# A two-block transformer kernel on one core: both halves of X in one product for the feature-major chunks, with a two-engine evacuation

## The chip, the cores and the metric

The kernel runs on one core of one Trainium2 chip. The core has TensorE (PE in the profile, with its weight loads as PEld), VectorE (DVE), ScalarE (ACT), GpSimd (POOL) and SyncE (SP, which here only issues DMAs). The metric is the device time of one execution in microseconds (us); lower is better. All names L823 and the like are line numbers of the kernel before.

## The reference

One sequence of 256 tokens, width 1024, goes through three layers, all in fp32. The parts that matter here:

```
mix = token_mixer(x)            # q,k,v of 8 forgetting heads (FoX) and 8 banded heads; w_out
  FoX: logit[t,s] = q_t.k_s/8 + cum[t] - cum[s], s <= t,  cum = cumsum(log_sigmoid(f + b_forget))
x   = layer_norm(a1*x + mix)
u   = x @ w_up ; u = conv over 3 tokens ; x = layer_norm(a1*x + (value*gelu(gate)) @ w_down)
h   = x @ w_in_even             # retention q,k,v,gate (4 heads) and MLA q,kv,gate (8 heads)
x   = layer_norm(a2*x + concat(ret_out, mla_out) @ w_out_even)
h   = x @ w_in_odd              # q,k,v,gate of 16 heads, rotary, causal within 256 tokens
x   = layer_norm(a2*x + (attention * silu(gate)) @ w_out_odd)
```

A softmax over s does not change when a term that depends on t alone is added to its logits, so `cum[t]` may be left out.

## The kernel before, in words

**Products in three parts.** An fp32 matrix product is made of three fp32r products: each operand is split into `hi` (its value rounded to fp32r by a ScalarE copy) and `lo` (value minus `hi`, a VectorE subtraction), and hi·hi, hi·lo and lo·hi are added up in PSUM (`three`, L823 to L825). The activations stand feature-major in `X_hi`, `X_lo` (8 tiles of 128 features by 256 tokens) and, for the input of an output projection, in `S_hi`, `S_lo`.

**Weights as a stream of pieces.** All weights are cut into 236 pieces, most of them 128x1024. SP loads a piece into one of 5 `raw` slots, ScalarE makes `w_hi` of it (L1117), VectorE `w_lo` (L1283), in a ring of 6, and TensorE uses it and frees it. A piece is split four pieces ahead of its use.

**Chunks.** Pieces form chunks (`chunks()`). A chunk of kind F makes 128 output features per piece with all 256 tokens as moving columns: 8 tiles times three matmuls of 256 columns, weights stationary. Up to two pieces share one PSUM bank. Kinds A and B have tokens as the stationary side and weights as 512 moving columns. `acc` has four banks for chunks, which rotate, and four more (`job`) for attention, transposes and retention. Before its first matmul a chunk waits until what its banks held has been evacuated (`chunk_waits`).

**Evacuation of an F chunk** is one step (`evac`): q and k of the first layer are copied by ScalarE (L1156); the convolution of a `w_up` chunk is two scaled ScalarE reads of PSUM (`taps`, L1125) and four VectorE multiply-adds that read PSUM (L1326); a rotary chunk is rotated by VectorE straight from PSUM (L1307 to L1318); a gate is a ScalarE tanh (L1171) and a VectorE multiply-add (L1346), both from PSUM.

**Attention** goes in pairs of heads through four steps each (`scores`, `soft`, `exp`, `norm`, then `pt`, `pv`, `yout`, `ylo`). For the FoX heads the term `cum[t] - cum[s]` enters as a second small product of 4 rows (L949) on top of q·k (L940). `cum` is computed in the `forget` evacuation: VectorE adds the bias (L1372), ScalarE does Abs, Exp and Ln (L1189), VectorE a minimum, a scan and four scalings (L1375 to L1383).

**The order** is one list (`plan`): half a piece of matmuls, the splits that belong to it, then at most one or two background steps. Each engine works through its own part of this list in order and waits on semaphores. A rotated chunk counts as ready four half pieces after its evacuation (`TURN_WAIT`).

Of the kernel before, what the change touches and what calls it, by code (L numbers as in the profile page):

```python
# [25 lines left out]
P = 128  # L26
# [40 lines left out]
def chunks():  # L67
# [29 lines left out]
    add("out1", "B", 8, "S", k8, "dve", ("norm", 0), ("w_out", k8, None))  # L97
# [11 lines left out]
    def mla(half):  # L109
        for a in (0, 1):  # L110
            add(f"mg{half}{a}", "F", 2, "X", k8, "dve", ("gate", 0, a),
                ("w_in_even", None, cols(MG + 512 * half + 256 * a, 256)), after_job=16 + 4 * half, at=2 + a)
# [45 lines left out]
    def moba_qk(half, a):  # L158
        for name, c0 in (("k", 1024), ("q", 0)):
            add(f"m{name}{half}{a}", "F", 2, "X", k8, "dve", ("rope", name, 1 - half, 2 * a, 64),  # L160
                ("w_in_odd", None, [c0 + 512 * half + 256 * a + 64 * h + i for h in range(4) for i in turn_perm]), after_ret=4)

    def moba_gate(half, a):
        add(f"mgt{half}{a}", "F", 2, "X", k8, "dve", ("gate", 1 - half, a),
            ("w_in_odd", None, cols(3072 + 512 * half + 256 * a, 256)), after_ret=4)
# [11 lines left out]
    add("out3", "B", 8, "S", k8, "dve", ("norm", 3), ("w_out_odd", k8, None))  # L177


    width = dict(F=1, A=2, B=4, C=4, Q1=4, Q2=4)  # L180
# [65 lines left out]
def cum_row(h):  # L246
    return 64 * (h % 2) + 32 * (h // 2 % 2)


# [8 lines left out]
def plan():  # L258

    order, given, pending, turning = [], set(), [], []  # L260
# [13 lines left out]

    def require(names):
        while not names <= given:
# [17 lines left out]
    def evacuate(c):  # L294
        emit(("evac", c))
        if CH[c]["evac"][0] in ("rope", "mla_q"):
            turning.append([CH[c]["name"], TURN_WAIT])
        else:
            given.add(CH[c]["name"])

    def run(name, rate, needs=lambda i: set(), early=0, between=(), tail=(), inside={}):
# [13 lines left out]
        for x, half in enumerate(halves):  # L315
# [25 lines left out]
            else:  # L341
                split_to(u + AHEAD + 1)
            for t in turning:
# [69 lines left out]
    split_to(1)  # L413

    for name in ("f", "kA0", "qA0", "vA", "kA1", "kB0"):
        run(name, 0)
# [10 lines left out]
    for j in range(2, FT + 2):  # L427
        if j < FT:
            run(f"up{j}", 0, tail=first if j == 2 else ())
# [53 lines left out]
    run("out3", 1, lambda i: {f"L3y{i}"})  # L483
# [59 lines left out]
for _name, _n in (("ident", P), ("causal", 3 * P), ("band", P), ("cumA", 4), ("cumB", 4),  # L543
# [6 lines left out]
def constants():  # L550
# [34 lines left out]
def build(nc, t):  # L585
    with ExitStack() as ctx:
# [9 lines left out]
        X_hi = sb("X_hi", [P, KT, S], F32R)  # L596
        X_lo = sb("X_lo", [P, KT, S], F32R)
# [77 lines left out]
        x_in = [sem(f"x_in{i}") for i in range(2 * NT)]  # L675
        pos_in, bf_in, conv_in = sem("pos_in"), sem("bf_in"), sem("conv_in")
# [23 lines left out]
        ROPES = [c for c, ch in enumerate(CH) if ch["evac"][0] in ("rope", "mla_q")]  # L700
# [1002 lines left out]
```

## Time and profile before

| | us |
|---|---|
| runs before (3): median, lowest, highest | 767.89, 767.82, 768.12 |
| the profiled execution's own time | 768.47 |
| its span | 766.7 |
| TensorE busy | 752.5 (98%) |
| VectorE busy | 528.8 (69%) |
| ScalarE busy | 382.5 (50%) |

The profiled execution is 0.58 us above the median of the runs. Its granted TensorE clock was 1.00 in nearly every stretch. Durations of matmuls overlap (each ends later than the next one starts), so the time that one matmul takes from TensorE is read as the distance between starts. Stages by time: first layer's q, k, v to 48 us, its attention and output projection to 150, `w_up` to 260, `w_down` to 330, the retention and MLA layer to 620, the last layer from there.

### The profile page before, as it was taken

To read this page: it belongs to the slowest core of one execution; us is meant where nothing else is said; L and a number is where in the kernel's file an instruction comes from. 1 tells how busy PE (TensorE), PEld (TensorE's weight loads), DVE (VectorE), ACT (ScalarE), POOL (GpSimd) and SP (SyncE) were. 2 spreads that over 40 slices of the span, in tenths; PEclk is the share of its full clock that TensorE was granted. 3 is DMA by queue.
4 is the path that set the end of the run, shared out by engine and by line. 5 is a ranking of instruction groups with operands and counts; after the bars stand their busy time and mean duration, and the time that the engine had idled before them with its cause. 6 is when DMAs were issued, how large, how long until landed. Compare 5 with 4: busy or idle time off the path is not lost.

```text
span 766.7 us, 12680 instructions
## 1 busy us (share of the span) xinstructions
PE 752.5 (98%) x4838; PEld 659.6 (86%) x4838; DVE 528.8 (69%) x940; ACT 382.5 (50%) x629; POOL 36.8 (5%) x50
## 2 busy tenths in 40 slices
PE   8999999999999999999999999999999999999995
PEld 8897777899999988799899777987788879988964
DVE  4654758697788854857686566965574587977766
ACT  5655763575655654156554444433443434565450
POOL 0000000021111200100000000000000010000001
PEclk9999999999999999999999999999999999999998
DMA  8852345456655685265536334553576617446402
GB/s 304 316 192 89 114 155 199 165 162 190 188 183 165 212 295 194 69 221 192 165 109 196 126 133 138 161 185 129 185 264 200 221 52 233 136 133 196 162 2 82
DMA packets 37580, 130.62 MB, mean 170 GB/s; under 512 B 4304, under 2 KB 4688, under 8 KB 37392
## 3 DMA queue, kind: packets, MB, share of 16 engines
q1 hardware_dynamic: 36144, 125.09, 49.2%
q0 software_dynamic: 1232, 4.46, 1.9%
q8 instruction: 39, 0.64, 0.3%
q10 hardware_dynamic: 144, 0.26, 0.1%
q14 instruction: 21, 0.17, 0.1%
HBM read 128.74 MB, written 1.05 MB: 169 GB/s over the span
## 4 chain that ended last, share of the span: by engine, by line
PE 95%; DVE 3%; issue 1%; DMA 1%; ACT 0%; DVEq 0%; SPq 0%
PE acc L823 28%; PE acc L825 27%; PE acc L824 27%; PE acc L940 2%; PE acc L959 2%; PE acc L979 2%; PE acc L998 1%; PE acc L938 1%; PE acc L1011 1%; PE acc L946 1%; DMA res<-in_x 1%; PE acc L972 0%; PE acc L1022 0%; PE acc L1037 0%; PE acc L1035 0%
## 5 line engine op out<-in xcount | busy, mean ns | idle before, releaser
L1283 DVE TENSOR_TENSOR w_lo<-raw,w_hi 128x1024 fp32r<-128x1024 f32 (+1 forms) x223 | 260.8, 1197 | 70.1 <-ACT w_hi L1117 69.3
L1117 ACT ACTIVATE w_hi<-raw 128x1024 fp32r<-128x1024 f32 (+1 forms) x223 | 224.4, 1034 | 88.8 <-PE acc L825 77.6
L823 PE MATMUL acc<-X_hi,w_hi 128*128 128x256 f32 x848 | 243.0, 287 | 0.6 <-DVE w_lo L1558 0.6
L824 PE MATMUL acc<-X_lo,w_hi 128*128 128x256 f32 x848 | 239.8, 283 | 0.0
L825 PE MATMUL acc<-X_hi,w_lo 128*128 128x256 f32 x848 | 239.8, 283 | 0.0
L823 PEld LDWEIGHTS acc<-X_hi,w_hi 128*128 128x128 f32 x848 | 162.5, 192 | 6.3 <-issue 5.1
L824 PEld LDWEIGHTS acc<-X_lo,w_hi 128*128 128x128 f32 x848 | 162.6, 192 | 0.5 <-issue 0.2
L825 PEld LDWEIGHTS acc<-X_hi,w_lo 128*128 128x128 f32 x848 | 162.5, 192 | 0.0
L823 PE MATMUL acc<-w_hi,S_hi 128*128 128x512 f32 x256 | 101.7, 397 | 1.3 <-DVE gate L1346 1.3
L824 PE MATMUL acc<-w_lo,S_hi 128*128 128x512 f32 x256 | 99.8, 390 | 0.0
L825 PE MATMUL acc<-w_hi,S_lo 128*128 128x512 f32 x256 | 99.7, 390 | 0.0
L823 PE MATMUL acc<-w_hi,X_hi 128*128 128x512 f32 (+1 forms) x192 | 74.4, 388 | 0.9 <-DVE w_lo L1283 0.9
L825 PE MATMUL acc<-w_hi,X_lo 128*128 128x512 f32 (+1 forms) x192 | 71.6, 373 | 0.0
L824 PE MATMUL acc<-w_lo,X_hi 128*128 128x512 f32 (+1 forms) x192 | 71.4, 372 | 0.0
L823 PEld LDWEIGHTS acc<-w_hi,S_hi 128*128 128x128 f32 x256 | 48.1, 188 | 13.0 <-issue 1.8
L825 PEld LDWEIGHTS acc<-w_hi,S_lo 128*128 128x128 f32 x256 | 48.1, 188 | 10.1
L824 PEld LDWEIGHTS acc<-w_lo,S_hi 128*128 128x128 f32 x256 | 48.1, 188 | 9.6 <-issue 0.2
L1326 DVE SCALAR_TENSOR_TENSOR v<-acc,cvp,v 128x255 f32<-128x255 f32 (+1 forms) x88 | 38.3, 477 | 20.9 <-ACT v L1125 20.1
L823 PEld LDWEIGHTS acc<-w_hi,X_hi 128*128 128x128 f32 x192 | 36.2, 189 | 9.4 <-issue 3.9
L1125 ACT ACTIVATE v<-acc,cvp 128x256 f32<-128x256 f32 x44 | 22.3, 561 | 42.6 <-PE acc L825 38.4
L825 PEld LDWEIGHTS acc<-w_hi,X_lo 128*128 128x128 f32 x192 | 36.2, 188 | 6.6
L824 PEld LDWEIGHTS acc<-w_lo,X_hi 128*128 128x128 f32 x192 | 36.3, 189 | 6.0 <-issue 0.5
(165 smaller groups left out, 795.7 us busy)
## 6 DMA issues: line engine op xcount, KB each, us to landing
raw<-in_w SPq DMA_DIRECT2D x225, 512.0 KB, 4.3
raw<-in_w SPq DMA_DIRECT2D x11, 256.0 KB, 3.1
gate<-in_ln_gain POOLq DMA_DIRECT2D x4, 512.0 KB, 5.2
gate<-in_ln_bias POOLq DMA_DIRECT2D x4, 512.0 KB, 5.7
res<-in_x SPq DMA_DIRECT2D x4, 256.0 KB, 4.2
gate<-in_bias SPq DMA_DIRECT2D x1, 1024.0 KB, 10.3
out<-res SPq DMA_DIRECT2D x4, 256.0 KB, 2.0
decay<-in_decay SPq DMA_DIRECT2D x1, 512.0 KB, 6.1
```

The lines of the kernel that those rows point to most:

```text
L823: nc.tensor.matmul(out, a_hi, b_hi, start=start, stop=False)
L824: nc.tensor.matmul(out, a_hi, b_lo, start=False, stop=False)
L825: return nc.tensor.matmul(out, a_lo, b_hi, start=False, stop=stop)
L938: nc.tensor.matmul(dst, qT[s][:, h, q], kT[s][:, h, 0:nk], start=True, stop=False)
L940: last[i] = nc.tensor.matmul(dst, qT[s][rows, h // 2, q], kT[s][rows, h // 2, 0:nk], start=True, stop=kind != "fox")
L946: last[i] = nc.tensor.matmul(dst, qpeT[rows, h // 2, q], kpeT[rows, 0, 0:nk], start=False, stop=True)
L959: last = nc.tensor.transpose(job[:, 2 + j % 2, b * P:(b + 1) * P], pr[:, j % 2, b * P:(b + 1) * P], ident)
L979: last = nc.tensor.matmul(job[i * HD:(i + 1) * HD, 3, q0:q0 + n], vv[s][:, tt, v], ptb[:, (j + i) % 2, b0:b0 + n], start=tt == 0, stop=tt ...
L1117: nc.scalar.activation(home(u, "hi")[:, 0:n], raw[:, u % RAW, 0:n], ACT.Copy).then_inc(hi_done, 1)
L1125: return [nc.scalar.activation(conv[j % 2][:, i, :], up[:, i * S:(i + 1) * S], ACT.Identity, scale=cvp[:, 2, i, j:j + 1], bias=cvp[:, 3, i ...
L1283: nc.vector.tensor_tensor(home(u, "lo")[:, 0:n], raw[:, u % RAW, 0:n], home(u, "hi")[:, 0:n].bitcast(F32), ALU.subtract).then_inc(lo_done, 1)
L1326: last = nc.vector.scalar_tensor_tensor(o, up[:, i * S:i * S + S - lag], cvp[:, 2 - lag, i, j:j + 1], o, ALU.mult, ALU.add)
```

## The change

- **Kind W.** `X_hi` and `X_lo` become the two halves of one tensor `X` (tile, half, token). For 48 chunks of two pieces (96 pieces) the kind F is replaced by W: per tile one matmul of 512 columns (`w_hi` on both halves) and one of 256 (`w_lo` on the hi half) instead of three of 256. A piece now has a bank of its own: columns 0 to 255 hold hi·hi and lo·hi, columns 256 to 511 hold hi·lo. A W chunk takes two of the four banks. The 48 chunks (in the code the same replacement stands in `ret_qk`, `moba_qk`, `moba_gate` and the second half of `mla`) are 6 of q and k of the first layer, 20 of `w_up`, 2 MLA gates, 8 of retention's q and k, 8 rotary and 4 gate chunks of the last layer. The single-piece chunks and the first two MLA gates stay F.
- **Evacuation of a W chunk.** At its end ScalarE copies the second halves of both banks to SBUF (`half`); half a piece later VectorE adds the first halves (`add_half`), which frees the banks. The convolution's taps and multiply-adds, the rotation and the tanh then read SBUF; a gate's tanh goes to another buffer and a further step (`gated`) multiplies.
- **FoX.** The product of 4 rows goes. The negated, scaled `cum` of the eight heads is written to DRAM and read back to all partitions by GpSimd's DMA queue (twice 512 KB), the causal mask is added by VectorE (`fox_mask`, four operations), and `soft` takes this as its bias. The scan moves behind the next chunk's third half piece (`forgotten`).
- **Order.** `rv0`, `out1`, `out3` start at bank 2 (`at=2`); `out3` takes its first two pieces token half by token half (`early=2`). At the start the second half of piece 0 is loaded and split before the last two parts of x. A ready rotary chunk counts five half pieces, not four.

```diff
-        add(f"{name}{half}", "F", 2, "X", k8, "act", ("copy_feat", name[0], s, 2 * half, 2),
+        add(f"{name}{half}", "W", 2, "X", k8, "dve", ("copy_feat", name[0], s, 2 * half, 2),
...
-        add(f"up{j}", "F", 2, "X", k8, "dve", ("conv", j),
+        add(f"up{j}", "W", 2, "X", k8, "dve", ("conv", j),
...
+    add("out3", "B", 8, "S", k8, "dve", ("norm", 3), ("w_out_odd", k8, None), at=2)
...
+        if CH[c]["kind"] == "W":
+
+            settle(9)
+            emit(("half", c))
+            if kind == "gate":
+                later.extend(([1, ("evac", c)], [2, ("tanh", c)], [3, ("gated", c), name]))
+            else:
+                later.append([1, ("evac", c)])
...
-        run(name, 0)
+        run(name, 0, inside={(1, 1): [("forgotten",)]} if name == "kA0" else {})
...
+            run(f"up{j}", 0, tail=first if j == 2 else (),
+                inside={(0, 1): [("taps", j - 1)], (1, 0): [("conv", j - 1)]} if j > 2 else {})
...
-    run("out3", 1, lambda i: {f"L3y{i}"})
+    run("out3", 1, lambda i: {f"L3y{i}"}, early=2)
...
+                elif kind == "W":
+                    wait_operand(step, ch, [("X", tt, part) for tt in range(NT)])
+                    for k in range(4 * part, 4 * part + 4):
+                        w = slice(k * P, (k + 1) * P)
+                        nc.tensor.matmul(acc[:, b0 + i, :], wh[:, w], X[:, k, :, :], start=k == 0, stop=False)
+                        last = nc.tensor.matmul(acc[:, b0 + i, 0:S], wl[:, w], X_hi[:, k, :], start=False, stop=k == KT - 1)
...
-                        elif kind == "fox":
-                            r = slice(cum_row(h), cum_row(h) + 4)
-                            last[i] = nc.tensor.matmul(dst, cumA[r, h // 4, q], cumB[r, h // 4, 0:nk], start=False, stop=True)
...
+            def half(c):
+
+                ch = CH[c]
+                e, b0, n = ch["evac"], ch["bank"], ch["n"]
+                wait_acc(act, c)
...
+                nc.scalar.activation(dst, acc[:, b0:b0 + n, S:2 * S], ACT.Copy).then_inc(half_copied, 1)
...
+            def add_half(c, whole):
+
+                ch = CH[c]
+                dve.wait_ge(half_copied, HALVED.index(c) + 1)
+                nc.vector.tensor_tensor(whole, whole, acc[:, ch["bank"]:ch["bank"] + ch["n"], 0:S], ALU.add).then_inc(evac_dve, 1)
+                dve.wait_ge(evac_dve, ch["count"])
...
+            def fox_mask():
+
+                dve.wait_ge(cum_out, 16 * 2)
+                dve.wait_ge(const_in, 16)
+                tri = const("causal")[:, 0:P].unsqueeze(1).to_broadcast([P, 4, P])
+                for i in range(2):
+                    nc.vector.tensor_tensor(corner[:, 4 * i:4 * i + 4, :], forgot[i][:, :, 0:P], tri, ALU.add)
+                    last = nc.vector.tensor_tensor(forgot[i][:, :, P:S], forgot[i][:, :, P:S], tri, ALU.add)
+                link(last)
...
+                    elif e[0] == "forget":
+                        pool.wait_ge(cum_ready, 1)
+                        pool.dma_start(cum_dram, fox[0:8, 2, :]).then_inc(cum_done, 16)
+                        pool.wait_ge(cum_done, 16)
+                        for i in range(2):
+                            pool.dma_start(forgot[i], cum_dram[4 * i:4 * i + 4, :].partition_broadcast(P)).then_inc(cum_out, 16)
```

VectorE, near the start, before: the splits of pieces 1 to 4, the forget chain, then the split of piece 5 and eleven more (`rtmp` holds the chain, `rot` the tables for the product of 4 rows):

```order
L1283 TENSOR_TENSOR w_lo<-raw,w_hi 128x1024 [waits hi_done] x4
L1372 TENSOR_SCALAR rtmp<-acc,small 128x256 [waits bf_in,w_used]
L1375 SCALAR_TENSOR_TENSOR rtmp<-rtmp 128x256 [waits ln_ready,z_ready]
L1378 SCALAR_TENSOR_TENSOR rtmp<-rtmp 128x256 [waits half_ready,dve_chain]
L1383 TENSOR_SCALAR rot<-rtmp,cst 128x256 [waits const_in,dve_chain]
L1383 TENSOR_SCALAR rot<-rtmp,cst 128x256 x3
L1283 TENSOR_TENSOR w_lo<-raw,w_hi 128x1024 [waits hi_done]
L1283 TENSOR_TENSOR w_lo<-raw,w_hi 128x1024 [waits w_used,hi_done] x11
```

The same place now (`kT0`, `qT0` are the destinations of the first two W chunks, kA0 and qA0):

```order
L1354 TENSOR_TENSOR w_lo<-raw,w_hi 128x1024 [waits hi_done] x4
L1467 TENSOR_SCALAR rtmp<-acc,small 128x256 [waits bf_in,w_used]
L1354 TENSOR_TENSOR w_lo<-raw,w_hi 128x1024 [waits hi_done]
L1475 SCALAR_TENSOR_TENSOR rtmp<-rtmp 128x256 [waits ln_ready,evac_dve]
L1478 SCALAR_TENSOR_TENSOR rtmp<-rtmp 128x256 [waits half_ready,dve_chain]
L1479 TENSOR_SCALAR rtmp<-rtmp 128x256 [waits dve_chain]
L1354 TENSOR_TENSOR w_lo<-raw,w_hi 128x1024 [waits w_used,hi_done]
L1367 TENSOR_TENSOR kT0<-kT0,acc 128x512 [waits half_copied,w_used]
L1354 TENSOR_TENSOR w_lo<-raw,w_hi 128x1024 [waits w_used,hi_done,evac_dve]
L1354 TENSOR_TENSOR w_lo<-raw,w_hi 128x1024 [waits w_used,hi_done]
L1367 TENSOR_TENSOR qT0<-qT0,acc 128x512 [waits half_copied,w_used]
```

The split of piece 5 has moved ahead of the scan, three scalings are gone, and the additions of the first two W chunks stand behind the splits of pieces 6 and 8.

VectorE in the `w_up` stage, one chunk before (`v0` is the convolution's buffer, `S_lo` a tile of the product h):

```order
L1283 TENSOR_TENSOR w_lo<-raw,w_hi 128x1024 [waits w_used,hi_done] x2
L1326 SCALAR_TENSOR_TENSOR v0<-acc,cvp,v0 128x255 [waits tap_act]
L1326 SCALAR_TENSOR_TENSOR v0<-acc,cvp,v0 128x255
L1326 SCALAR_TENSOR_TENSOR v0<-acc,cvp,v0 128x254 [waits dve_chain]
L1326 SCALAR_TENSOR_TENSOR v0<-acc,cvp,v0 128x254
L1447 TENSOR_TENSOR S_lo<-v0,S_hi 128x256 [waits h_hi]
```

And now:

```order
L1367 TENSOR_TENSOR rtmp<-rtmp,acc 128x512 [waits half_copied,w_used]
L1354 TENSOR_TENSOR w_lo<-raw,w_hi 128x1024 [waits w_used,hi_done,evac_dve]
L1417 SCALAR_TENSOR_TENSOR v1<-rtmp,cvp,v1 128x255 [waits tap_act]
L1417 SCALAR_TENSOR_TENSOR v1<-rtmp,cvp,v1 128x255
L1417 SCALAR_TENSOR_TENSOR v1<-rtmp,cvp,v1 128x254 [waits dve_chain]
L1417 SCALAR_TENSOR_TENSOR v1<-rtmp,cvp,v1 128x254
L1354 TENSOR_TENSOR w_lo<-raw,w_hi 128x1024 [waits w_used,hi_done]
L1554 TENSOR_TENSOR S_lo<-v0,S_hi 128x256 [waits h_hi]
```

One operation has come in (L1367), and the two splits stand on either side of the multiply-adds, which now read `rtmp` in SBUF.

TensorE at the start, from the end of kA0 into qA0, now (two rows per tile, 512 columns and then 256; before, three of 256 in the same place, and only waits for the splits):

```order
L901 MATMUL acc<-X,w_hi 128x512
L902 MATMUL acc<-X,w_lo 128x256
L901 MATMUL acc<-X,w_hi 128x512
L902 MATMUL acc<-X,w_lo 128x256
L901 MATMUL acc<-X,w_hi 128x512 [waits t_lo,lo_done,evac_dve]
L902 MATMUL acc<-X,w_lo 128x256
L901 MATMUL acc<-X,w_hi 128x512
L902 MATMUL acc<-X,w_lo 128x256
L901 MATMUL acc<-X,w_hi 128x512
L902 MATMUL acc<-X,w_lo 128x256
```

The wait for evac_dve is that of qA0 (bank 0, which the forget chunk held). `vA`, the next chunk, waits for evac_dve of kA0 (banks 2 and 3), which is the addition L1367 above; before, `vA` waited for the evacuation of the forget chunk and of kA0 by ScalarE.

## Rows read from the trace of the kernel before

**Rows 1.** The page: busy time of each engine.
```profile
PE 752.5 (98%) x4838; PEld 659.6 (86%) x4838; DVE 528.8 (69%) x940; ACT 382.5 (50%) x629; POOL 36.8 (5%) x50
```

**Rows 2.** The page's chain that ended last, by engine; then the longest wait of TensorE.
```profile
PE 95%; DVE 3%; issue 1%; DMA 1%; ACT 0%; DVEq 0%; SPq 0%
...
PE acc L823 <- DVE gate L1346: 1.3, 1, 1.3
```

**Rows 3.** Timeline of TensorE in w_up: start, duration, engine, line; 57 rows, first and last.
```profile
229.74 0.28 PE L824 MATMUL acc<-X_lo,w_hi 128*128 128x256 f32 x1
...
236.46 0.28 PE L823 MATMUL acc<-X_hi,w_hi 128*128 128x256 f32 x1
```

**Rows 4.** The same in w_down, 512 columns: first and last of 16 rows.
```profile
310.20 0.39 PE L823 MATMUL acc<-w_hi,S_hi 128*128 128x512 f32 x1
...
313.60 0.39 PE L823 MATMUL acc<-w_hi,S_hi 128*128 128x512 f32 x1
```

**Rows 5.** Timeline of TensorE: scores of a FoX pair, then of a banded pair.
```profile
74.22 0.49 PE L940 MATMUL acc<-kT,qT 64*128 64x128 f32 x4
...
75.70 0.70 PE L949 MATMUL acc<-rot 4*128 4x256 f32 x4
76.33 0.50 PE L823 MATMUL acc<-w_hi,X_hi 128*128 128x512 f32 x1
...
82.34 0.93 PE L940 MATMUL acc<-kT,qT 64*128 64x128 f32 x8
83.20 0.50 PE L823 MATMUL acc<-w_hi,X_hi 128*128 128x512 f32 x1
```

**Rows 6.** Groups by form: busy us, mean ns, idle before and its releaser.
```profile
L1290 DVE TENSOR_TENSOR X_lo<-acc,X_hi 128x512 fp32r<-128x512 f32 x16 | 10.8, 690 | 7.2 <-ACT X_hi L1137 7.1
L1171 ACT ACTIVATE gate<-acc 128x512 f32<-128x512 f32 x8 | 4.8, 599 | 20.5 <-PE acc L825 20.5
```

**Rows 7.** Timeline of VectorE in w_up, one chunk, the next one's addition of angles.
```profile
217.06 2.35 DVE L1283 TENSOR_TENSOR w_lo<-raw,w_hi 128x1024 fp32r<-128x1024 f32 x2
220.79 1.78 DVE L1326 SCALAR_TENSOR_TENSOR v<-acc,cvp,v 128x255 f32<-128x255 f32 x4 [1.38 <-ACT v L1125]
222.49 0.42 DVE L1447 TENSOR_TENSOR S_lo<-v,S_hi 128x256 fp32r<-128x256 f32 x1
...
245.86 1.41 DVE L1463 SCALAR_TENSOR_TENSOR qT<-qT 128x512 f32<-128x512 f32 x2
...
248.11 2.36 DVE L1283 TENSOR_TENSOR w_lo<-raw,w_hi 128x1024 fp32r<-128x1024 f32 x2
```

**Rows 8.** Timeline at the start: VectorE, then ScalarE, then TensorE's first matmul of vA.
```profile
17.48 0.49 DVE L1372 TENSOR_SCALAR rtmp<-acc,small 128x256 f32<-128x256 f32 x1 [1.85 <-DMA small<-in_b_forget]
20.78 0.42 DVE L1375 SCALAR_TENSOR_TENSOR rtmp<-rtmp 128x256 f32<-128x256 f32 x1 [2.81 <-ACT rtmp L1189]
21.24 0.69 DVE L1378 TENSOR_TENSOR_SCAN rtmp<-rtmp 128x256 f32<-128x256 f32 x1
...
20.70 2.01 ACT L1117 ACTIVATE w_hi<-raw 128x1024 fp32r<-128x1024 f32 x2
...
24.74 0.47 PE L823 MATMUL acc<-w_hi,X_hi 128*128 128x512 f32 x1 [0.94 <-DVE w_lo L1283]
```

**Rows 9.** Timeline at the first attention pair: VectorE's bias and last norm, TensorE's transposes.
```profile
46.11 1.22 DVE L1395 SCALAR_TENSOR_TENSOR gate<-gate,cst 128x1024 f32<-128x1024 f32 x1
...
55.50 0.35 DVE L1420 TENSOR_SCALAR pr<-pr,small 128x256 f32<-128x256 f32 x1
...
55.27 1.18 PE L959 MATMUL acc<-cst,pr 128*128 128x128 f32 x6
```

**Rows 10.** The page's DMA issues: a broadcast of 512 KB (KB each, us to landing).
```profile
gate<-in_ln_gain POOLq DMA_DIRECT2D x4, 512.0 KB, 5.2
```

**Rows 11.** Timeline in the last layer: VectorE's last norm of a pair, TensorE's transposes.
```profile
656.71 0.35 DVE L1420 TENSOR_SCALAR pr<-pr,small 128x256 f32<-128x256 f32 x1
...
658.01 0.82 PE L959 MATMUL acc<-cst,pr 128*128 128x128 f32 x6
```

More of the change, by code:

```diff
@@ L96, in chunks @@
                 ("w_in", None, cols(c0 + P * unit, P)))
-    add("out1", "B", 8, "S", k8, "dve", ("norm", 0), ("w_out", k8, None))
+    add("out1", "B", 8, "S", k8, "dve", ("norm", 0), ("w_out", k8, None), at=2)
     add("up01", "A", 4, "X", k8, "act", ("up_tok",),
@@ L176, in chunks @@
     moba_gate(1, 1)
-    add("out3", "B", 8, "S", k8, "dve", ("norm", 3), ("w_out_odd", k8, None))
-    width = dict(F=1, A=2, B=4, C=4, Q1=4, Q2=4)
+    add("out3", "B", 8, "S", k8, "dve", ("norm", 3), ("w_out_odd", k8, None), at=2)
+    width = dict(F=1, W=2, A=2, B=4, C=4, Q1=4, Q2=4)
     at, held, n_act, n_dve, u = 0, [None] * 4, 0, 0, 0
@@ L258, in plan @@
 def plan():
-    order, given, pending, turning = [], set(), [], []
+    order, given, pending, turning, later = [], set(), [], [], []
     state = dict(hi=0, lo=0, credit=0)
@@ L273, in background, with settle @@
             given.update(gives)
+    def settle(n):
+        for x in list(later):
+            x[0] -= n
+            if x[0] <= 0:
+                later.remove(x)
+                emit(*x[1:])
     def require(names):
+        if not names <= given and not pending[0][0] <= given:
+            settle(9)
         while not names <= given:
@@ L428, in plan @@
         if j < FT:
-            run(f"up{j}", 0, tail=first if j == 2 else ())
+            run(f"up{j}", 0, tail=first if j == 2 else (),
+                inside={(0, 1): [("taps", j - 1)], (1, 0): [("conv", j - 1)]} if j > 2 else {})
+        if j == FT:
+            settle(9)
+            emit(("taps", j - 1))
+            emit(("conv", j - 1))
         if j <= FT:
@@ L700, in build @@
         ROPES = [c for c, ch in enumerate(CH) if ch["evac"][0] in ("rope", "mla_q")]
+        HALVED = [c for c, ch in enumerate(CH) if ch["kind"] == "W"]
+        GATED = [ch["name"] for c, ch in enumerate(CH) if ch["kind"] == "W" and ch["evac"][0] == "gate"]
         GATE = [c for c, ch in enumerate(CH) if ch["evac"][0] == "gate"]
@@ L856, in mm @@
                 elif i == 0 and part == 0:
-                    chunk_waits(pe, c, range(b0, b0 + (2 if kind == "A" else 1)))
+                    chunk_waits(pe, c, range(b0, b0 + (2 if kind in ("A", "W") else 1)))
                 if u == 0 and part == 0:
@@ L1142, in evac @@
                 kind = e[0]
-                if kind in ("rope", "norm"):
+                if kind in ("rope", "norm") or ch["kind"] == "W":
                     return
@@ L1254, in _ @@
                     yout(step[1])
+                elif step[0] == "half":
+                    half(step[1])
+                elif step[0] == "tanh":
+                    tanh(step[1])
+                elif step[0] == "taps":
+                    up_taps(step[1])
                 elif step[0] == "gelu":
@@ L1302, in rope @@
                     dve.wait_ge(qn_copied, 1 + ch["evac"][1])
+                whole = ch["kind"] == "W"
+                if whole:
+                    x = rope_whole(c)
+                    add_half(c, x)
                 wide = rope_width(c) == 256
@@ L1342, in evac @@
                     rope(c)
+                elif kind == "gate" and ch["kind"] == "W":
+                    add_half(c, gateT[:, e[1], 2 * e[2]:2 * e[2] + 2, :])
+                elif kind == "copy_feat":
+                    add_half(c, feat_dest(e))
                 elif kind == "gate" and len(e) == 3:
@@ L1644, in lay_out @@
     b_forget = np.zeros((P, 1), np.float32)
-    for h in range(8):
-        for r in (0, 1):
-            at = cum_row(h) + 2 * (h // 4) + r
-            forget[:, at] = a["w_in"][0][:, FA + h]
-            b_forget[at, 0] = a["b_forget"][0][h]
+    forget[:, 0:8] = a["w_in"][0][:, FA:FA + 8]
+    b_forget[0:8, 0] = a["b_forget"][0]
     for u, (c, i) in enumerate(PIECES):
```

174 lines of the change are left out of this document (106 added, 68 removed).

## The prediction

> **What bounds the kernel now.** I read the page's busy times first: TensorE is busy in 98% of the span, VectorE in 69%, ScalarE in half [rows 1]. The chain of waits agrees: 95% of it is TensorE, 3% VectorE [rows 2], most of that at the start and in the last layer norm. In the list of waits TensorE's longest is one of 1.3 us on a gate's evacuation, at `out3` [rows 2]. So a microsecond of matmuls taken away is a microsecond of time, as long as the other engines keep up, and any new wait of TensorE is paid in full.
>
> What one matmul takes must be read from the distance of starts, not from the durations, which overlap. In `w_up` 57 rows of 256 columns start from 229.74 to 236.46: 6.72 / 56 = 0.120 us each [rows 3]. With 512 columns 16 rows start from 310.20 to 313.60: 3.40 / 15 = 0.2267 us [rows 4]. The difference, 0.1067 us, is 256 columns at 2.4 GHz; the rest, 0.0133 us, is paid once per matmul whatever its length.
>
> **Part 1, kind W.** The columns stay the same (3 x 256 = 512 + 256); one matmul of three goes. A step over one tile took 3 x 0.120 = 0.360 us and now takes 0.2267 + 0.120 = 0.3467 us. 96 pieces times 8 tiles are 768 steps: 768 x 0.0133 = **10.2 us** less (up 4.3, retention, MLA and q, k of the first layer 3.4, last layer 2.6). A chunk falls from 5.76 to 5.55 us. The bounds: no gain at all, if a matmul of 512 columns followed by one of 256 with other weights lost what is saved; 10.2 by the rows. I take the rows, since both lengths show the same fixed part.
>
> The Trainium skill ("TensorE: Matmul & The Clock Gate", section "Back-to-back issue gap") gives N / 2.4 + 2.5 ns for a warm matmul. The trace has N / 2.4 + 13.3 ns at both lengths. By the page this part would bring 768 x 0.0025 = 1.9 us; the rows decide, and the page's case is a rival below.
>
> **Part 2, FoX without its second product.** From the first q·k matmul of a FoX pair to the matmul behind the scores it takes 76.33 - 74.22 = 2.11 us; a banded pair, which has the q·k part alone, takes 83.20 - 82.34 = 0.86 us [rows 5]. The new FoX scores are of the banded form. Four pairs: 4 x 1.25 = **5.0 us** less. The skill ("TensorEngine Tiling (Array Packing)", "Key Properties") says that a change of tiling mode drains TensorE; the four rows against eight that all run in 0.86 us agree.
>
> **Part 3, out3's wait.** It starts at banks 2 and 3, and its first two pieces run their first token half before the second, so the last gate's banks are needed half a piece group later. **1.3 us** less [rows 2].
>
> **Part 4, the start.** TensorE's first matmul of vA starts at 24.74, after a wait for the split of piece 5 [rows 8]. That split now stands before the scan, but vA (banks 2, 3) now waits for the addition of kA0, which stands behind the scan and the split of piece 6. The chain: ScalarE is free of the logarithm at 20.70, as now, since it hangs on the b_forget DMA that VectorE waits for until 17.48 [rows 8]; hi of piece 5 to 21.7 (2.01 us for two), its lo to 22.9 (2.35 us for two [rows 7]), minimum, scan and one scaling 1.6 (0.42 and 0.69 [rows 8], the scaling put at the minimum's 0.42, with gaps) to 24.5, lo of piece 6 to 25.65, the addition 0.65 [rows 6] to 26.3. vA starts about 1.6 us later than now. Since Part 1 already counts 0.4 us saved ahead of it, this costs **2.0 us**. Bounds: the present 24.74 (if b_forget lands some 1.5 us earlier, its issue comes sooner) and 27.5. Loading the second half of piece 0 before half of x moves a split of 0.7 us forward and two transposes back by 256 KB of DMA; I take nothing.
>
> **Part 5, the first pair.** VectorE does the bias of the banded heads until 47.3 [rows 9], just before kB0 ends. Now four masks of 512 columns (4 x 0.62 = 2.5) stand ahead of it, and kB0's addition behind it. Counted from kB0's end, the bias is done at 2.9, the addition at 3.5, and softmax, two splits and two norms take the same 4.9 us as now: the last norm is ready at 8.4. TensorE comes to its transposes after three half pieces and 0.86 us of scores and one more half piece, at 6.4, and waits 2.0; now it waits 0.36 there (1.11 us for transposes that take 0.75, [rows 9]). Cost **1.6 us**: this pair gives most of its 1.25 back. The DRAM round trip of cum starts at 24.5; two broadcasts at 5.2 us each [rows 10] and a short write end before 37, the masks are due at 46: hidden. If it took over 20 us it would show here.
>
> **Part 6, VectorE in w_up.** One chunk costs it two splits (2.28, starts apart), four multiply-adds (1.74), a split of h (0.34) [rows 7]: 4.36 of 5.76 us. The addition reads PSUM and SBUF as the X split does, 0.69 us, 0.61 from start to start [rows 6]: 4.97 of 5.55. It also waits in two new places, for ScalarE's copy (0.6 [rows 6]) and taps. ScalarE has copy, gelu, h and a split before the taps, all done 3.6 us after the chunk's end; VectorE comes there about 3.9. So it follows some 0.7 us late and no wait grows. The banks are free 2.2 us after the chunk's end, wanted after 5.55. Bounds of the addition: 0.42 (the split of h, half its width [rows 7]) and 1.15 (a split of 1024 columns); with 1.15 a chunk costs 5.5, still under 5.55. Cost nothing. But the four blocks of angles (one took 248.11 - 245.86 = 2.25 us, [rows 7]; I put the others at 1.0 to 1.6) now add up against a slack of 0.58 us per chunk instead of 1.4: VectorE is some 3 us late at the last chunk. Behind it stand the whole chain add, taps, convolution, gelu, product, h split (about 6.5 us) before `w_down`'s fifth piece can be split, which TensorE wants 10.9 us after. **0.8 us** (0 to 2).
>
> **Part 7, small waits.** In the last layer a pair's last norm ends at 657.06, TensorE's transposes start at 658.01 [rows 11]: 0.95 us of slack. Now a gate's addition precedes and a gate's multiplication (0.61) enters this stretch, and its steps are 4 x 0.05 shorter: 0.3 us of wait once. The rotations of the last layer and of retention read SBUF after an addition, 24 W chunks with 0.61 more on VectorE; elsewhere their followers have several us. With a few like it: **0.6 us**.
>
> **Sum.** -10.2 - 5.0 - 1.3 + 2.0 + 1.6 + 0.8 + 0.6 = -11.5 us. Against the profiled execution's own 768.47 (span 766.7): 757.0. That execution is 0.58 above the runs' median of 767.89, so **756.4 us** is forecast for a median.
>
> **Rivals.**
> *All waits hidden (chance 0.17).* The chain at the start goes by the earlier b_forget, and ScalarE and VectorE keep up. Then -10.2 - 5.0 - 1.3 - 0.3: about 751.5. For it: TensorE hardly waits now with VectorE at 69%. Against it: the chain of Part 4 rests on rows one by one.
> *VectorE is late more often (0.20).* Its load in W stages is about 90%, and each attention pair has under 1 us of slack [rows 11]. If 20 of the places where TensorE waits on a norm, a bank or a split cost 0.25 us each, 5 us come on top: 761.5.
> *The fixed part is not saved (0.05).* A wide matmul and a narrow one alternate, and the gap of 0.0133 grows to what three had, or the page's 2.5 ns is what a matmul really adds: 10.2 shrinks to 1.9, so 764.7.
> *Slower: two banks instead of four (0.05).* A W chunk holds two banks, so chunk c+2 starts only when copy and addition of c are done, both in order behind splits. If VectorE's work per chunk exceeds TensorE's 5.55 us, all 48 chunks run at VectorE's pace. From (5.81 - 5.55) x 48 = 12.5 us the gain is gone; at 6.0 us per chunk the time is 756.4 + 48 x 0.45 = 778. That needs 1.0 us more per chunk than the rows give. Speaks for it that the multiply-adds' reads move to SBUF, where ScalarE reads too; against it, a split from SBUF costs what one from PSUM does per column (1.15 for 1024, 0.61 for 512).
> *Does not do what it says:* the order shows the matmuls gone; only their price is open.
>
> **How the numbers follow.** Forecast 0.53 with its own range 753.5 to 759.5. The range for 8 in 10 takes in most of the first two rivals: 751 to 762. A measurement of this kernel tells a change of 0.2% (1.5 us) from none. Everything but the slower rival lies below 766.4, apart from a tail of the third: faster 0.92, same 0.03, slower 0.05.
>
> **What would show it.** Starts in a W chunk 0.227 and 0.120 us apart, a chunk in 5.55 us; FoX scores in 0.86; no wait before out3; vA's first matmul at 26.3 with a wait of 3.0 on the addition of kA0 (L1367); 2.0 us before the first transposes; a wait under 2 us at w_down's fifth piece; VectorE at 74 to 76% of the span. I am wrong if W steps take over 0.35 us, if TensorE's busy share falls below 96%, or if waits on L1367 recur through w_up.

## The result, and the profile after

| | before | changed |
|---|---|---|
| runs: median (lowest to highest), us | 767.86 (767.68 to 768.12) | 771.12 (770.62 to 773.04) |
| profiled execution: own time, span | 768.47, 766.7 | 771.35, 769.6 |

The ratio is 1.0047, with a 95% interval from 1.0029 to 1.0064. The forecast was 756.4: the changed kernel is slower by 3.3 us where it was to be faster by 11.5. I had given slower a chance of 0.05. Two of the three signs of being wrong that I had named are there: W steps take over 0.35 us, and waits on L1367 come back in w_up. The third, a TensorE share below 96%, is not.

The page's busy times and the first entries of its chain, of the changed kernel:

```profile
PE 747.1 (97%) x4038; PEld 617.3 (80%) x4038; DVE 571.0 (74%) x989; ACT 407.3 (53%) x671; POOL 45.6 (6%) x53
...
PE 75%; DVE 15%; ACT 4%; issue 3%; DMA 1%; SPq 1%; DVEq 0%; POOL 0%; ACTq 0%
```

The 800 matmuls are gone, TensorE's share fell only a little, but VectorE's share of the chain went from 3% [rows 2] to 15%. TensorE's longest waits show where (us in total, times, longest):

```profile
PE acc L901 <- DVE rtmp L1367: 3.9, 3, 1.8
PE acc L988 <- DVE pr L1524: 3.3, 2, 2.1
PE acc L851 <- DVE w_lo L1354: 1.4, 1, 1.4
PE acc L1027 <- DMA res<-in_x: 1.2, 1, 1.2
...
PE acc L851 <- DVE kT L1367: 0.7, 1, 0.7
```

Both kernels run the same products of weights in the same order, so the start of one product in both traces gives the lead or lag there. This ledger holds the prediction's sum against these positions (us; W is kind W's own share of the forecast):

| stretch | start in both | change, forecast | change, measured |
|---|---|---|---|
| to vA's first product | 24.74, 25.18 | +1.6 (W -0.4) | +0.44 |
| to 144.75 of before: 4 FoX pairs, 4 W chunks | 144.75, 141.41 | -4.3 (W -0.9) | -3.78 |
| to 282.55: w_up, start of w_down, 20 W chunks | 282.55, 284.72 | -3.5 (W -4.3) | **+5.51** |
| to 722.26: 22 W chunks | 722.26, 722.54 | -4.1 (W -4.7) | -1.89 |
| out3, to the last product | 757.32, 760.18 | -1.3 | **+2.58** |

Three things are off: w_up by 9.0 us, out3 by 3.9, and each W chunk saves half of what it should.

**A W step.** First matmul of 512 columns of the first and of the last step of one chunk, then the same of a later chunk:

```profile
198.82 0.40 PE L901 MATMUL acc<-X,w_hi 128*128 128x512 f32 x1
...
204.12 0.40 PE L901 MATMUL acc<-X,w_hi 128*128 128x512 f32 x1
...
227.04 0.41 PE L901 MATMUL acc<-X,w_hi 128*128 128x512 f32 x1
...
232.26 0.40 PE L901 MATMUL acc<-X,w_hi 128*128 128x512 f32 x1
```

5.30 / 15 = 0.3533 us per step in the first, 5.22 / 15 = 0.348 in the second. Nearly all undisturbed chunks are like the first: a chunk starts 5.65 us after the one before. The step saves 0.0067 us, not 0.0133. From start to start the wide matmul takes 0.236 us and the narrow one 0.117 (means over w_up from 159 to 221 us), where the rows before gave 0.2267 in w_down [rows 4] and 0.120; so the wide one loses more than the step does.

**VectorE in w_up**, one chunk and the next one's addition, and GpSimd's product beside it:

```profile
208.52 0.67 DVE L1367 TENSOR_TENSOR rtmp<-rtmp,acc 128x512 f32<-128x512 f32 x1
209.23 1.23 DVE L1354 TENSOR_TENSOR w_lo<-raw,w_hi 128x1024 fp32r<-128x1024 f32 x1
210.37 1.79 DVE L1417 SCALAR_TENSOR_TENSOR v<-rtmp,cvp,v 128x255 f32<-128x255 f32 x4
212.07 1.22 DVE L1354 TENSOR_TENSOR w_lo<-raw,w_hi 128x1024 fp32r<-128x1024 f32 x1
213.21 0.97 DVE L1554 TENSOR_TENSOR S_lo<-v,S_hi 128x256 fp32r<-128x256 f32 x1
214.10 0.67 DVE L1367 TENSOR_TENSOR rtmp<-rtmp,acc 128x512 f32<-128x512 f32 x1
```

```profile
212.69 1.20 POOL L1744 TENSOR_TENSOR v<-v 128x256 f32<-128x256 f32 x1 [4.37 <-ACT v L1294]
```

No idle time stands in these rows: VectorE is full, 14.10 - 8.52 = 5.58 us per chunk where I had 4.97. Of the 0.61 us more, 0.10 is the addition (0.71 from start to start, where I had 0.61) and 0.55 the h split (L1554), less 0.04 at the multiply-adds. The h split takes 0.97 us, where it had 0.42 [rows 7], for the same operands. It is ready at about 213.2, in the middle of GpSimd's product, which itself takes 1.20. The numbers fit if only one of the two can read at a time: the product, issued at 212.69, waits until the weight split ends at 213.2, then takes 0.74 to 213.9, and the h split has its 0.34 after that. In the kernel before, the product ran beside the multiply-adds, which read one operand from PSUM, and took its 0.74:

```profile
232.66 0.74 POOL L1625 TENSOR_TENSOR v<-v 128x256 f32<-128x256 f32 x1 [5.02 <-ACT v L1229]
```

At 5.58 against 5.65 VectorE still keeps pace, but has nothing left for the angles. TensorE waits 1.41 and 1.82 us, and after the second wait runs at half its clock (windows: PE busy, granted clock, DMA share, GB/s):

```profile
242.00:246.00 4.00, 3.76 (x22) 1.00 0.69 208
246.00:248.00 2.00, 0.42 (x2) 1.00 0.25 102
248.00:250.00 2.00, 2.00 (x9) 0.50 0.15 27
250.00:251.00 1.00, 1.00 (x4) 0.50 0.83 303
251.00:252.00 1.00, 1.00 (x6) 0.79 0.42 168
```

That chunk takes 7.22 us instead of 5.65, 1.6 us beside the wait. The same happens in out3:

```profile
739.50 0.90 PE L988 MATMUL acc<-cst,pr 128*128 128x128 f32 x3 [2.12 <-DVE pr L1524]
740.33 1.65 PE L972 MATMUL acc<-kT,qT 64*128 64x128 f32 x8
```

The eight scores take 1.65 us, against 0.93 elsewhere. VectorE before that wait, and ScalarE:

```profile
731.21 0.42 DVE L1515 CUSTOM_DVE_ANT_0 pr<-acc,cst 128x256 f32<-128x256 f32 x1
...
733.09 1.23 DVE L1354 TENSOR_TENSOR w_lo<-raw,w_hi 128x1024 fp32r<-128x1024 f32 x1 [1.45 <-ACT w_hi L1160]
734.23 0.69 DVE L1374 SCALAR_TENSOR_TENSOR gate<-ryb,gate 128x512 f32<-128x512 f32 x1
...
737.56 1.22 DVE L1354 TENSOR_TENSOR w_lo<-raw,w_hi 128x1024 fp32r<-128x1024 f32 x1 [1.65 <-ACT w_hi L1160]
...
739.10 0.35 DVE L1524 TENSOR_SCALAR pr<-pr,small 128x256 f32<-128x256 f32 x1
```

```profile
732.01 1.04 ACT L1160 ACTIVATE w_hi<-raw 128x1024 fp32r<-128x1024 f32 x1
...
736.49 1.99 ACT L1160 ACTIVATE w_hi<-raw 128x1024 fp32r<-128x1024 f32 x2
```

VectorE stands idle twice, 1.45 and 1.65 us, for a `w_hi` that ScalarE has only begun, with the gate's multiplication and two norms queued behind. So out3 lost its old wait of 1.3 us [rows 2] and got a longer one.

### The profile page after: what moved, and what is told of

The parts are those of the page before. It is cut to its first block, busy times and chain, and to the rows that moved or that the text cites. A ratio compares the mean times of both kernels' runs of the same rounds, so it can differ in the third digit from the quotient of the medians.

```text
span 769.6 us, 11240 instructions
## 1 busy us (share of the span) xinstructions
PE 747.1 (97%) x4038; PEld 617.3 (80%) x4038; DVE 571.0 (74%) x989; ACT 407.3 (53%) x671; POOL 45.6 (6%) x53
## 3 DMA queue, kind: packets, MB, share of 16 engines
q0 software_dynamic: 1552, 5.51, 2.2%
## 4 chain that ended last, share of the span: by engine, by line
PE 75%; DVE 15%; ACT 4%; issue 3%; DMA 1%; SPq 1%; DVEq 0%; POOL 0%; ACTq 0%
PE acc L851 16%; PE acc L853 15%; PE acc L852 15%; PE acc L901 13%; PE acc L902 6%; DVE w_lo L1354 5%; DVE v L1417 4%; ACT w_hi L1160 2%; PE acc L972 2%; PE acc L988 2%; DVE rtmp L1367 2%; PE acc L1008 1%; DMA raw<-in_w 1%; DVE S_lo L1554 1%; PE acc L970 1%
## 5 line engine op out<-in xcount | busy, mean ns | idle before, releaser
L901 PE MATMUL acc<-X,w_hi 128*128 128x512 f32 x768 | 276.4, 403 | 3.9 <-DVE rtmp L1367 3.9
L902 PE MATMUL acc<-X,w_lo 128*128 128x256 f32 x768 | 216.2, 281 | 0.0
L901 PEld LDWEIGHTS acc<-X,w_hi 128*128 128x128 f32 x768 | 145.0, 189 | 43.7 <-DVE rtmp L1367 4.9
L902 PEld LDWEIGHTS acc<-X,w_lo 128*128 128x128 f32 x768 | 145.8, 190 | 0.5 <-issue 0.2
L851 PE MATMUL acc<-w_hi,X 128*128 128x512 f32 (+1 forms) x192 | 74.4, 387 | 0.7 <-DVE kT L1367 0.7
L853 PE MATMUL acc<-w_hi,X 128*128 128x512 f32 (+1 forms) x192 | 71.6, 373 | 0.0
L852 PE MATMUL acc<-w_lo,X 128*128 128x512 f32 (+1 forms) x192 | 71.5, 372 | 0.0
L851 PEld LDWEIGHTS acc<-w_hi,X 128*128 128x128 f32 x192 | 36.2, 189 | 9.5 <-issue 2.8
L853 PEld LDWEIGHTS acc<-w_hi,X 128*128 128x128 f32 x192 | 36.2, 188 | 6.6
L852 PEld LDWEIGHTS acc<-w_lo,X 128*128 128x128 f32 x192 | 36.2, 189 | 6.0 <-issue 0.5
L1417 DVE SCALAR_TENSOR_TENSOR v<-rtmp,cvp,v 128x255 f32<-128x255 f32 (+1 forms) x80 | 35.0, 478 | 1.9 <-ACT v L1168 1.2
L1168 ACT ACTIVATE v<-rtmp,cvp 128x256 f32<-128x256 f32 x40 | 21.9, 595 | 25.7 <-DVE rtmp L1367 25.7
```

The costliest lines, as they stand in the source:

```text
L851: nc.tensor.matmul(out, a_hi, b_hi, start=start, stop=False)
L852: nc.tensor.matmul(out, a_hi, b_lo, start=False, stop=False)
L853: return nc.tensor.matmul(out, a_lo, b_hi, start=False, stop=stop)
L901: nc.tensor.matmul(acc[:, b0 + i, :], wh[:, w], X[:, k, :, :], start=k == 0, stop=False)
L902: last = nc.tensor.matmul(acc[:, b0 + i, 0:S], wl[:, w], X_hi[:, k, :], start=False, stop=k == KT - 1)
L1168: return [nc.scalar.activation(conv[j % 2][:, i, :], up[:, i * S:(i + 1) * S], ACT.Identity, scale=cvp[:, 2, i, j:j + 1], bias=cvp[:, 3, i ...
```

## The experiments

Each kernel below ran beside the kernel before on one chip; its ratio is to that. The medians of the kernel before were 768.03, 768.20 and 767.79 us in the three groups.

**h_early.** The h split's place in the order:

```diff
-                inside={(0, 1): [("taps", j - 1)], (1, 0): [("conv", j - 1)]} if j > 2 else {})
+                inside={(0, 1): [("taps", j - 1)], (1, 0): [("conv", j - 1), ("h_split", j - 2)]} if j > 2 else {})
...
-        emit(("h_split", j - 2))
+        if not 2 < j < FT:
+            emit(("h_split", j - 2))
```

> The changed kernel, with one step of the order moved: in w_up the split of h(j-2) stands right behind the convolution of chunk j-1, ahead of GpSimd's product of j-1, not behind VectorE's second weight split. Theory A (VectorE waits for the SBUF access that GpSimd's product holds): the h split falls from 0.97 to 0.42 us, VectorE's work per chunk from 5.58 to 5.03 us, TensorE's waits of 1.41 and 1.82 us on the addition in w_up and the half-clock stretch behind them go, most of the wait of 1.38 us in w_down too: 764.5 to 766. Rival B (the addition and the angle blocks alone overload VectorE, or the h split is slow by itself in this layout): the split stays near 0.97 or the waits stay; 769.5 to 771.5.

765.75 us (763.92 to 767.10), ratio 0.9970 (0.9958 to 0.9981): 5.4 us under the changed kernel. The waits in w_up but the first (0.8) are gone. Its VectorE in w_up:

```profile
206.03 0.69 DVE L1368 TENSOR_TENSOR rtmp<-rtmp,acc 128x512 f32<-128x512 f32 x1
207.27 1.23 DVE L1355 TENSOR_TENSOR w_lo<-raw,w_hi 128x1024 fp32r<-128x1024 f32 x1 [0.55 <-ACT w_hi L1161]
208.41 1.79 DVE L1418 SCALAR_TENSOR_TENSOR v<-rtmp,cvp,v 128x255 f32<-128x255 f32 x4
210.11 0.42 DVE L1555 TENSOR_TENSOR S_lo<-v,S_hi 128x256 fp32r<-128x256 f32 x1
```

```profile
206.31 0.74 POOL L1745 TENSOR_TENSOR v<-v 128x256 f32<-128x256 f32 x1 [4.92 <-ACT v L1295]
```

The same operation on the same operands takes 0.42 us when the product is elsewhere, and the product 0.74, here beside the addition, which reads one operand from PSUM. VectorE has idle time again. Where it is behind, it now takes 5.03 us from one addition to the next, as expected. Theory A holds. The wait in w_down stayed (1.5), which A had wrong: it hangs on the chain behind the last chunk and VectorE's delay from the angles. The four blocks still put VectorE some 4 us behind here, over eight chunks (49.2 us between additions, against 45.2 at TensorE's pace), and in w_up no wait of TensorE comes of it.

**angles_late.** The angles leave w_up:

```diff
-        if 14 <= j < 22 and j % 2 == 0:
-            emit(("angles", j // 2 - 7))
...
-    run("down", 0, tail=turn_x(2, 0), inside={(8, 0): [("sines",)]})
+    run("down", 0, tail=turn_x(2, 0), inside={**{(g + 6, 0): [("angles", g)] for g in range(4)}, (11, 0): [("sines",)]})
```

> The changed kernel with the four blocks of angles moved from w_up into w_down (one each ahead of pieces 6 to 9, the sines three pieces later). Both theories: VectorE's steady 5.58 us per chunk stands just under TensorE's 5.65, so without the blocks no backlog arises and the waits of 1.41 and 1.82 us and the half-clock stretch go (some 5 us); the h split stays at 0.97. The wait of 1.38 at w_down's fifth piece is shorter or gone. 765 to 767. If instead the steady load of w_up by itself is too much, waits on the addition remain in w_up and the time stays above 769.

764.50 us (763.29 to 765.40), ratio 0.9953 (0.9941 to 0.9965): 6.6 us under the changed kernel. The h split stays at 0.96 to 0.97 through w_up, VectorE at 5.58 us per chunk:

```profile
207.90 0.97 DVE L1552 TENSOR_TENSOR S_lo<-v,S_hi 128x256 fp32r<-128x256 f32 x1
```

Yet no wait remains in w_up but the first (0.8), and the one in w_down is gone too. So the long waits of w_up took both, the collision and the angles: with either alone none of them arises. The wait in w_down takes the angles alone.

**quads.** Order of the matmuls in a W piece's half:

```diff
                     for k in range(4 * part, 4 * part + 4):
                         w = slice(k * P, (k + 1) * P)
                         nc.tensor.matmul(acc[:, b0 + i, :], wh[:, w], X[:, k, :, :], start=k == 0, stop=False)
+                    for k in range(4 * part, 4 * part + 4):
+                        w = slice(k * P, (k + 1) * P)
                         last = nc.tensor.matmul(acc[:, b0 + i, 0:S], wl[:, w], X_hi[:, k, :], start=False, stop=k == KT - 1)
```

> The changed kernel, W pieces with four matmuls of 512 columns and then four of 256 per half piece, not alternating. Theory C (alternation between 512 and 256 columns costs the missing 0.0067 us per step): steps average 0.3467 us, 28 chunks outside w_up gain 0.107 us each (3 us); in w_up VectorE takes that gain back in longer waits: 767.5 to 769. Rival D (the 0.0067 has another cause): steps stay at 0.3533 or turn longer, 771 or more.

769.92 us (the median of five executions, 768.67 to 771.79; a sixth, in which matmuls took some 5.5 times as long, came to 4181 and is left out; the only trace is of that one). Ratio 1.0030 (1.0018 to 1.0042). That is 1.2 under the changed kernel, between the two expectations, and the step can't be read; `combo_quads` below has a trace for it.

**no_early.** out3's first two pieces in the usual order:

```diff
-    run("out3", 1, lambda i: {f"L3y{i}"}, early=2)
+    run("out3", 1, lambda i: {f"L3y{i}"})
```

> The changed kernel with out3's first two pieces in the usual order (both token halves of a piece together), out3 still starting at bank 2. Theory E (the early order issues the high and low split of a piece together, so VectorE stands idle on ScalarE's w_hi with a gate's multiplication and norm queued behind it): TensorE's wait of 2.12 us at the transposes of out3 and the half-clock stretch behind it (about 1.1 us) go: 767.5 to 769. Rival F (the new steps of the gate, tanh and multiplication, by themselves make the norm late): a wait of over 1.5 us stays at the transposes, 770.5 to 771.5.

767.14 us (766.88 to 769.26 in 11 executions), ratio 0.9991 (0.9982 to 1.0000): 4.0 us under the changed kernel, a little more than expected. No wait remains in out3. `at=2` is still in, so starting at bank 2 was enough to take away the old wait of 1.3 us. In its trace the wait in w_down was 2.8 us, in the changed kernel's 1.4: that place varies between executions. Two of its waits in w_up and w_down:

```profile
247.32 0.50 PE L901 MATMUL acc<-X,w_hi 128*128 128x512 f32 x1 [1.84 <-DVE rtmp L1367]
...
272.52 0.50 PE L851 MATMUL acc<-w_hi,S_hi 128*128 128x512 f32 x1 [2.81 <-DVE w_lo L1354]
```

After the first the granted clock stayed at 1.00, after the second it fell to 0.50 for 3.4 us.

**Four together, and one more edit on each.** `combo` holds h_early, angles_late and no_early.

> The three moves together: h split behind the convolution, angles in w_down, out3 without the early order. If the three losses are separate (w_up and w_down 6.0 us by positions with the angles moved, out3 3.9 us), the time is 771.1 - 6.6 - 4.0 = 760.5 us, and the move of the h split adds nothing since VectorE already keeps up. If the wait in w_down comes back (2.8 us in one run) it is 762 to 763.

760.38 us (759.54 to 760.87), ratio 0.9898 (0.9883 to 0.9913). The losses are separate and add up as expected.

> The three moves, and W pieces with four matmuls of 512 and then four of 256 columns per half piece. Theory C (alternation costs 0.0067 us per step): steps of 0.3467 us, 5.1 us less than without: 755.5. Rival D (another cause): as without, 760.5, or more.

758.61 us (758.22 to 759.48), ratio 0.9878 (0.9863 to 0.9892): 1.8 us less than combo, between the two expectations. Its matmuls, in fours:

```profile
703.85 1.09 PE L900 MATMUL acc<-X,w_hi 128*128 128x512 f32 x4
704.78 0.64 PE L903 MATMUL acc<-X,w_lo 128*128 128x256 f32 x4
705.25 1.09 PE L900 MATMUL acc<-X,w_hi 128*128 128x512 f32 x4
```

Four steps take 1.40 us here; over whole chunks, which now start 5.61 us apart, a step takes 5.61 / 16 = 0.3506 us. By that alternation accounts for 0.0027 of the missing 0.0067 us, by the time for 1.8 / 768 = 0.0023. The four wide ones take 0.93, 0.2325 each, still not 0.2267, and the narrow ones 0.47, 0.1175 each: the rest stands at the wide matmul with X moving and weights stationary, and its cause stays open.

`combo_bias`: only the FoX mask stays ahead of the first pair.

```diff
-    emit(("bias",))
+    emit(("mask",))
     attention(range(0, 16))
...
-        run(name, 1.25)
+        run(name, 1.25, inside={(0, 1): [("bias",)]} if name == "qB0" else {})
```

> The three moves, and the bias of the banded heads moved from ahead of the first attention pair into chunk qB0; only the FoX mask stays ahead of it. If VectorE's queue of mask and bias makes the first norm late, TensorE's wait of 1.2 us at the first pair goes: 759.3. If it is kB0's addition and the softmax chain itself, the wait stays: 760.5.

759.58 us (758.40 to 760.39), ratio 0.9888 (0.9871 to 0.9904), 0.8 under combo, inside the spread of the runs; but the wait is what the trace shows, and it fell from 1.2 to 0.22:

```profile
54.71 0.55 PE L987 MATMUL acc<-cst,pr 128*128 128x128 f32 x3 [0.22 <-DVE pr L1523]
```

`combo_x`: all of x is loaded ahead of the second half of piece 0, and piece 0 is split after the transposes, as in the kernel before.

```diff
-        if i == 1:
-            split_to(1)
+    split_to(1)
...
-                        if (tt, q) == (0, 1):
-                            sp.dma_start(raw[:, 0, 512:1024], t["w"][0, :, 512:1024]).then_inc(landed[0], 16)
...
+                    sp.dma_start(raw[:, 0, 512:1024], t["w"][0, :, 512:1024]).then_inc(landed[0], 16)
```

> The three moves, and the start as before the change: all of x loaded ahead of the second half of piece 0, which is split after the transposes. The first product starts at 8.4 us, not 9.8. If vA's start is set by VectorE's chain (forget, split, addition of kA0), its wait grows from 0.7 to some 1.5 us and the time stays at 760.5; if it is set by TensorE's own work, 759.7.

762.07 us (761.26 to 762.70), ratio 0.9921 (0.9906 to 0.9935), 1.7 **slower** than combo, which neither theory had. By the two traces 0.83 us of it arises at vA, and 1.17 at a wait on a ScalarE operation in the retention layer (at 342 us). First product, first product of vA, and VectorE's bias and addition of kA0:

```profile
8.99 0.35 PE L848 MATMUL acc<-X,w_hi 128*128 128x256 f32 x1
...
26.03 0.50 PE L848 MATMUL acc<-w_hi,X 128*128 128x512 f32 x1 [1.78 <-DVE kT L1364]
```

```profile
17.32 0.48 DVE L1464 TENSOR_SCALAR rtmp<-acc,small 128x256 f32<-128x256 f32 x1 [1.33 <-DMA small<-in_b_forget]
...
25.30 0.68 DVE L1364 TENSOR_TENSOR kT<-kT,acc 128x512 f32<-128x512 f32 x1
```

In the changed kernel the same four rows:

```profile
9.76 0.36 PE L851 MATMUL acc<-X,w_hi 128*128 128x256 f32 x1
...
25.18 0.51 PE L851 MATMUL acc<-w_hi,X 128*128 128x512 f32 x1 [0.71 <-DVE kT L1367]
```

```profile
16.48 0.47 DVE L1467 TENSOR_SCALAR rtmp<-acc,small 128x256 f32<-128x256 f32 x1
...
24.44 0.68 DVE L1367 TENSOR_TENSOR kT<-kT,acc 128x512 f32<-128x512 f32 x1
```

With the changed load order the first product comes 0.8 later and vA 0.85 earlier, because VectorE's chain begins with a bias that need not wait for b_forget's DMA: SyncE issues that load at 10.1 us, in combo_x at 12.1. The wait in the retention layer isn't shown to be the start's: `best`, which shares combo's start, has one of 1.1 there too, and `best_early`, with the same code up to there, has none. So the start accounts for some 0.8 of the 1.7 us, and the rest stays open.

**A version that beats both.** `best` is combo with quads and the moved bias. `best_early` is best with out3's early order back, but the low split of a piece half a piece group behind its high split:

```diff
-                if part == 1:
+                if part == 1 and name == "out3":
+                    split_to(u + AHEAD + 1, ("hi",))
+                    split_to(u + AHEAD, ("lo",))
+                elif part == 1:
                     split_to(u + AHEAD + 1)
```

> All moves that gained, together: h split behind the convolution, angles in w_down, out3 without the early order, four wide and then four narrow matmuls, the banded heads' bias in qB0. By sum from the single runs: 760.4 - 1.8 - 0.8 = 757.8 us. If the 1.2 us of the first pair is really gained back (by positions in one profile), 757.4.

758.08 us (757.78 to 758.58), ratio 0.9874 (0.9859 to 0.9889), as summed.

> As before, but out3 keeps the early order (token half by token half for its first two pieces), with the high split of a piece issued half a piece group ahead of its low split. Theory E (what hurt was VectorE standing idle on a just issued w_hi, not the order of the matmuls): no wait over 0.3 us in out3, 757.8. If the order itself hurts, a wait of 1.5 to 2.8 us at out3's transposes and a half-clock stretch are back: 760 to 761.5.

757.72 us (757.54 to 758.01), ratio 0.9870 (0.9853 to 0.9886), with the early order and no wait over 0.3 us in out3; VectorE there goes from softmax straight into the gate's multiplication:

```profile
721.34 0.42 DVE L1519 CUSTOM_DVE_ANT_0 pr<-acc,cst 128x256 f32<-128x256 f32 x1
...
721.68 0.69 DVE L1378 SCALAR_TENSOR_TENSOR gate<-ryb,gate 128x512 f32<-128x512 f32 x1
```

So theory E holds in its exact form: the order of the matmuls was harmless, the joined splits were not. Nor does the order gain anything: `best` and `best_early` take the same time for out3, and their traces differ by 1.0 us at the wait in the retention layer alone. Their executions overlap; both are about 10 us under the kernel before.

## Why the prediction was wrong, by its own steps

- **Part 6, VectorE in w_up at "cost nothing" (0.8 us for the angles): the step that failed.** Measured 5.51 + 20 x 0.107 = 7.7 us. The addition was priced nearly right (0.71 us from start to start, I had 0.61). What I did not see is that the second weight split, moved behind the convolution, pushes the h split into GpSimd's product, and that the two hold each other up: +0.55 us per chunk. That took VectorE from 4.97 to 5.58 and its slack from 0.6 to 0.07 us per chunk, less than the angles. h_early gives 5.4 us back, angles_late 6.6. Without the collision the part's own working comes out near: h_early has 5.03 us per chunk (I had 4.97), VectorE some 4 us late at the end (3), and 1.5 us of wait in w_down (0 to 2). I had listed both lines of the order and read only durations from them, not what runs beside what. The rule stood in the Trainium skill ("SBUF — State Buffer", "Who interferes with whom"): a `tensor_tensor` with both inputs in SBUF contends with GpSimd's reads, and the one that issues second is blocked until the first is done. The traces agree: 0.97 against 0.42 for one, 1.20 against 0.74 for the other, and the same split beside no product at 0.42.
- **A term that no part had: the clock.** In the changed kernel the granted clock is at half (1.2 GHz) for 3.4 us after the waits of 1.82 and 2.12 us, and full after those of 1.41 and 1.38. The length of the wait doesn't decide it alone: waits of 1.84 us (no_early), 1.78 (combo_x) and 1.89 (h_early, at its start) left it full, those of 2.12 and more (h_early, angles_late, no_early) did not. It cost 1.6 us at the first, and about 1.5 at the second (0.7 of it in the eight scores), on top of the waits. I priced waits at their length.
- **Part 3, out3, -1.3.** The old wait went, as forecast, but out3 came out 2.6 us slower. I spoke of the banks, which were right (no_early keeps `at=2` and has no wait in out3), and did not follow what `early=2` does to the splits. no_early (-4.0) and best_early (all kept, splits apart, no wait) show it.
- **Part 1, -10.2.** The mechanism is right, the size is half: 48 x 0.107 = 5.1 us. That both lengths have the same fixed part was taken from w_down, where activations stand still and weights move; with weights standing still and narrow matmuls between, a step takes 0.0067 more than that. Its bound "no gain at all" was there, and my middle should have been nearer to it. The alternation makes up 0.0023 to 0.0027 of it (combo_quads); the rest is open. The rival by the 2.5 ns of the Trainium skill ("TensorE: Matmul & The Clock Gate", "Back-to-back issue gap") had 1.9 us, an estimate from that page's figure; measured are 5.1, so neither it nor my sum is right.
- **Part 4, +2.0.** The chain was right: with the old load order vA starts at 26.03, I had said 26.3. But the new load order, at which I put nothing, lets b_forget's load be issued 2 us and its bias start 0.8 us earlier; vA starts at 25.18. Its bound named just this.
- **Part 5, +1.6.** 1.21 us, by the mechanism forecast; moving the bias takes 1.0 of it away.
- **Part 2, -5.0.** Right: the scores of a pair take 49.85 - 48.99 = 0.86 us, four pairs 5.0, and the DRAM round trip never shows.
- **Part 7, +0.6.** From 283 to 722 us: -1.89 + 22 x 0.107 = +0.5. The size is right; no run takes its waits apart. It speaks of 24 W chunks there, where there are 22.

Of the rivals, the one that VectorE is late more often (0.20) was nearest in kind, but I priced 20 small waits of 0.25 us; there were four of 1.38 us and more in w_up, w_down and out3, and the two longest cost the clock as well. (The first rival's terms add up to -16.8, so to 751.1 and not 751.5.) The slower rival (all W chunks at VectorE's pace) needed 5.81 us per chunk; VectorE reached 5.58, and the time was lost without it.

## What to carry to other kernels

When an edit moves an instruction, look not only at what it waits for but at what runs beside it in its new place, above all VectorE operations with two SBUF inputs against GpSimd. Slack per period is the number that decides: VectorE with 0.6 us of slack per chunk carried the angles through w_up without a long wait, with 0.07 it did not; so the blocks that come every other chunk are to be held against the slack, not against the mean. And a split issued on one engine right behind the one on another that it waits for makes a queue of two engines; keep a step between them.

## What the runs showed of the hardware that was not expected

- VectorE's split of 128x256 from two SBUF tensors takes 0.42 us alone and 0.97 when a GpSimd product is running; GpSimd's takes 0.74 alone and 1.20 when VectorE's split is running (1.54 in h_early, where it meets a weight split).
- A matmul of 512 columns takes 0.2267 us from start to start with activations stationary. With weights stationary and X moving it takes 0.236 when it alternates with one of 256 columns (which then takes 0.117), and 0.2325 in fours. In a few chunks (222 to 232 and 254 to 260 us) wide and narrow together take 0.347, the forecast 0.3467. This is open.
- In one of six executions of quads matmuls took some 5.5 times their time: 1.28 us for 512 columns and 0.64 for 256 from start to start, while VectorE's weight split kept its 1.22. That trace has no record of the granted clock. It was not seen again, not in combo_quads or best either.
- The granted clock fell to half after every wait of TensorE of 2.12 us and more (up to 2.81), and after one of 1.82, but not after those of 1.78, 1.84 and 1.89.
